# Memory's rows taken into the seven products of the output projection, its token blocks loaded by GpSimd's queue, a new order at its seam, and the rows' squares at other steps

## The reference

```python
h = rms_norm(x, pre_norm)
proj = h @ w_in_a                                  # 1024 -> 3072 + 1536 + 512
p, gate, mq = proj[..., :3072], proj[..., 3072:4608], proj[..., 4608:]
b_gate, c_gate, u = split(p, 3)
mix = b_gate * conv3(c_gate * u)                   # 1024 wide
mem_o = attention(mq, rms_norm(mem, mem_norm) @ w_mem_kv)   # 4 heads, 512 wide
y = (concatenate([mix, mem_o]) * silu(gate)) @ w_out         # 1536 -> 1024
out = x + rms_norm(y, post_norm)
```

## Time and profile before

| what | value |
|---|---|
| three runs, median (lowest to highest) | 2201.29 us (2198.6 to 2203.97) |
| profiled execution, its own time | 2198.74 us |
| its span, first to last instruction | 2197.0 us |
| mean granted TensorE clock | 0.999 |
| instructions | 26714 |
| busy: PE, PEld | 2172.3 us (99%), 1802.3 us (82%) |
| busy: DVE, ACT, POOL | 1174.7 us (53%), 737.3 us (34%), 131.8 us (6%) |
| DMA | 488.47 MB, mean 222 GB/s |
| chain that ended last | PE 91%, DVE 4%, DMA 2%, ACT 2%, issue 1% |

### The profile page before, as it was taken

How to read it: one execution, slowest core, us unless ns; L and a number is a source line. 1 busy time by engine, 2 the same in 40 slices (tenths; PEclk the granted TensorE clock), 3 DMA queues, 4 the chain that set the end, 5 groups by cost and what they waited for, 6 DMA issues and landing times.

```text
span 2197.0 us, 26714 instructions
## 1 busy us (share of the span) xinstructions
PE 2172.3 (99%) x9916; PEld 1802.3 (82%) x9916; DVE 1174.7 (53%) x1847; ACT 737.3 (34%) x1329; POOL 131.8 (6%) x207
## 2 busy tenths in 40 slices
PE   9999999999999999999999999999999999999998
PEld 7888788888888888888888878888887788888887
DVE  7668667643335352254334337585754755555554
ACT  5444333411221341221114334535442533333332
POOL 0000000000000000011000000101010100000000
PEclk9999999999999999999999999999999999999999
DMA  6887777677676777888768666666668633344332
GB/s 240 296 318 274 278 271 271 236 237 282 229 247 211 269 250 261 285 263 300 258 211 274 226 215 202 216 196 216 201 200 303 220 121 109 121 134 134 128 116 73
DMA packets 148336, 488.47 MB, mean 222 GB/s; under 512 B 16688, under 2 KB 16720, under 8 KB 144880
## 3 DMA queue, kind: packets, MB, share of 16 engines
q1 hardware_dynamic: 120672, 387.50, 50.3%
q0 software_dynamic: 27536, 99.27, 14.1%
HBM read 350.38 MB, written 136.33 MB: 222 GB/s over the span
## 4 chain that ended last, share of the span: by engine, by line
PE 91%; DVE 4%; DMA 2%; ACT 2%; issue 1%; SPq 0%; DVEq 0%; ACTq 0%
PE banks L1547 30%; PE banks L1548 30%; PE banks L1549 30%; DVE hop_lo L1171 1%; DMA slots<-w_split 1%; PE banks L1644 1%; ACT hop_hi L891 1%; ACT probs L952 0%; DVE x_in L1157 0%; DMA raws<-in_w_in 0%; DMA raws<-in_w_kv 0%; DVE rmax L1320 0%; DVE pt_lo L1335 0%; DVE slots L1199 0%; ACT slots L846 0%
## 5 line engine op out<-in xcount | busy, mean ns | idle before, releaser
L1547 PE MATMUL banks<-hop_hi,slots 128*128 128x512 f32 x2632 | 1028.4, 391 | 9.6 <-DMA slots<-w_split 4.0
L1548 PE MATMUL banks<-hop_lo,slots 128*128 128x512 f32 x2632 | 1025.2, 390 | 0.0
L1549 PE MATMUL banks<-hop_hi,slots 128*128 128x512 f32 x2632 | 1024.8, 389 | 0.0
L1547 PEld LDWEIGHTS banks<-hop_hi,slots 128*128 128x128 f32 x2632 | 494.6, 188 | 117.5 <-DMA slots<-w_split 7.0
L1549 PEld LDWEIGHTS banks<-hop_hi,slots 128*128 128x128 f32 x2632 | 494.4, 188 | 103.3
L1548 PEld LDWEIGHTS banks<-hop_lo,slots 128*128 128x128 f32 x2632 | 494.7, 188 | 100.3
L1199 DVE TENSOR_TENSOR slots<-raws,slots 128x512 fp32r<-128x512 f32 x156 | 106.8, 690 | 154.9 <-ACT slots L846 154.4
L1251 DVE TENSOR_TENSOR u<-banks,u 128x512 f32<-128x512 f32 x54 | 37.2, 690 | 227.6 <-PE banks L1549 227.6
L902 ACT ACTIVATE s<-banks 128x512 f32<-128x512 f32 x94 | 56.2, 598 | 299.5 <-PE banks L1549 298.7
L846 ACT ACTIVATE slots<-raws 128x512 fp32r<-128x512 f32 x156 | 96.7, 625 | 151.6 <-PE banks L1549 130.9
L846 ACT ACTIVATE slots<-st_w 128x512 fp32r<-128x512 f32 x144 | 90.2, 626 | 149.0 <-PE banks L1549 119.2
(11 more groups left out here) (170 smaller groups left out, 2035.9 us busy)
## 6 DMA issues: line engine op xcount, KB each, us to landing
slots<-w_split SPq DMA_DIRECT2D x406, 512.0 KB, 3.7
w_split<-slots SPq DMA_DIRECT2D x140, 512.0 KB, 3.4
raws<-in_w_in SPq DMA_DIRECT2D x86, 256.0 KB, 4.5
x_in<-in_x_t SPq DMA_DIRECT2D x16, 1024.0 KB, 6.9
g_kept<-mix POOLq DMA_DIRECT2D x32, 512.0 KB, 6.5
raws<-g_kept SPq DMA_DIRECT2D x64, 256.0 KB, 3.9
row<-in_x POOLq DMA_DIRECT2D x24, 512.0 KB, 6.0
x_zb<-in_x POOLq DMA_DIRECT2D x22, 512.0 KB, 4.1
```

Of the source, the lines that this page charges most:

```text
L1547: nc.tensor.matmul(dst, a, c, start=first, stop=False, skip_group_check=True)
L1548: nc.tensor.matmul(dst, a, d, start=False, stop=False, skip_group_check=True)
L1549: return nc.tensor.matmul(dst, b, c, start=False, stop=last, skip_group_check=True)
```

## The change

What it does:

- Memory's four blocks of rows go through the seven products: each has two blocks more (`HB` = 2), 18 matmuls instead of 12. M0, M1, `add_memory` and the adding of its PSUM bank are gone. A token block has 768 columns instead of 512 (`BLOCK`), holds the gated memory output in its last 256, and is kept so in `g_kept`.
- The seven split sums of memory's rows are made in macro 2, one each three steps from step 15 to 57 (`MW_AT`), and kept in `mw_kept`. In the output stage those of R1, R6, R7, R4 stay in SBUF; those of R5, R3, R2 are loaded anew in every pair by SP (`load_stream`), into one buffer of two blocks. R5 takes memory's blocks first, R3 after two others, R2 after three.
- The output stage has three slots for units (`out_slots`) instead of four, and builds them three steps ahead. Token blocks have one buffer each (`out_raws`); sums are made in place.
- Token blocks of all pairs but the first are loaded by POOL (`load_block`), between its stores and residual loads, of which there are two buffers instead of three. ACT evacuates straight into `mix`, when the tile before is finished.
- At the seam all seven operands go through two staging blocks; three of them (R7, R2, R4) are split after the output stage has begun. In its first pair ACT saves R1, R5, R6 in free PSUM banks and copies them later.
- Squares of rows: steps 20, 27, 34, 41 and 54, 60, 66, 72; each row is loaded one step after the square before it. Memory's two squares: steps 108 and 118 of macro 2, its root and inverse there too. The sums of `w_out`'s rows start 14 steps later.

The core of the diff:

```diff
-OUT_ORDER = [R1, R5, R6, R3, M0, R7, R2, M1, R4]
+OUT_STEPS = [(ALL_PAIRS + j, r) for j in range(OUT_PAIRS) for r in range(PRODUCTS)]
+HB = MH // 2
+BLOCK = (HK + HB) * P
+OUT_SLOTS = 3
+STREAMED = {R5: 0, R3: 2, R2: 3}
-SUMS_AFTER = list(range(6, 6 + 2 * HK + 1, 2))
+SUMS_AFTER = list(range(8, 8 + 2 * HK + 1, 2))
+MW_AT = [15 + 3 * n + 3 * (n // PRODUCTS) for n in range(HB * PRODUCTS)]
+MEM_SQUARES = (108, 118)
...
         def prefetch_steps(m):
-            return (41, 52, 63), (69, 80, 91)
+            return ((20, 27, 34, 41), 43, 63), ((54, 60, 66, 72), 74, 91)
...
+            def load_stream(j, r):
+                n = STREAM.index((j, r))
+                for k in range(HB):
+                    if n:
+                        sp.wait_ge(mw_used, HB * (n - 1) + k + 1)
+                    sp.dma_start(mw_stream[:, k, :, :].bitcast(f32), mw_kept[r, k]).then_inc(mw_stream_dma[k], 16)
...
-                    if step == squares - 11:
+                    if step == squares[0] - 6:
                         load_row(tile, 0)
                     for c in range(1, SUB):
-                        if step == squares + 3 * c - 2:
+                        if step == squares[c - 1] + 1:
                             load_row(tile, c)
...
+            for j in range(OUT_PAIRS):
+                if j:
+                    if j + 1 < OUT_PAIRS:
+                        load_block(pool, ALL_PAIRS + j + 1, X21)
+                    store_tile(2 * j - 1)
+                    load_residual(2 * j + 1)
+                if j + 1 < OUT_PAIRS:
+                    for block in (X11, X12, X22) if j else OUT_BLOCKS:
+                        load_block(pool, ALL_PAIRS + j + 1, block)
+                if j == 0:
+                    load_residual(0)
+                    load_residual(1)
+                store_tile(2 * j)
+                if j + 1 < OUT_PAIRS:
+                    load_residual(2 * j + 2)
...
+                if p == ALL_PAIRS and r == R3:
+                    mix_free(act, p, 1)
+                    for first, later, done in ((R6, R3, u2_done), (R5, R7, p5_done), (R1, R2, s1_done)):
+                        act.wait_ge(done, seven_to(p))
+                        nc.scalar.activation(temp(p, later), first_temp[first], ACT.Copy).then_inc(first_mixed, 1)
...
-                    if i == PAIRS - 1 and m + 1 == OUT and r != R4:
-                        operand_hi(OUT, r)
+                    if i == PAIRS - 1 and m + 1 == OUT and r in (R1, R5, R7, R2):
+                        operand_hi(OUT, {R1: R1, R5: R5, R7: R6, R2: R3}[r])
...
+                if n in (0, 2, 3):
+                    operand_hi(OUT, {0: R7, 2: R2, 3: R4}[n])
...
+                if n in (0, 1, 3, 4):
+                    operand_lo(OUT, {0: R3, 1: R7, 3: R2, 4: R4}[n])
...
-                for k in range(HK):
+                tiles = list(range(HK))
+                if m >= OUT:
+                    at = STREAMED.get(r, HK)
+                    tiles[at:at] = range(HK, HK + HB)
+                for k in tiles:
                     w = [a[:, k * P:(k + 1) * P] for a in unit(u)]
-                    op = product(dst, w, [a[:, r, k, :] for a in (hop_hi, hop_lo)], k == 0 and r in starts, k == HK - 1)
+                    y = [a[:, r, k, :] for a in (hop_hi, hop_lo)] if k < HK else memory_rows(p, r, k - HK)
+                    op = product(dst, w, y, k == tiles[0] and r in (R1, R5, R2), k == tiles[-1])
```

476 lines of the change are left out of this document (282 added, 194 removed).

## The result

| kernel | median, us (range) | ratio to before, 95% interval | profiled execution, span |
|---|---|---|---|
| before | 2201.29 (2198.6 to 2203.97) | 1 | 2198.74, 2197.0 |
| changed | 2190.34 (2187.47 to 2196.44) | 0.9948 [0.9932, 0.9963] | 2188.14, 2186.3 |

A forecast was written before the change was run, and what follows sets the result against it. PE, busy in 99% of the span, was taken as the bound, so the number of matmuls sets the time. Terms -21.8 + 5.7 - 6.4 = -22.5 gave 2176.2 (profiled) or 2178.8 (median); forecast 2178, range 2172 to 2184, chance 0.58.

The forecast's parts named there:

- 1. The matmuls: Output stage: 6 fewer matmuls a pair, 96 in all, at 0.2268 us each, -21.8 us.
- 2. Steady state: The 16 pairs of the output stage: added work stays hidden behind PE, pair 28.6 us, cost 0.
- Rival C: Output stage: R5's evacuation late in every pair, each of 15 pairs losing 1 us, 2193; chance 0.06.
- 3. The seam: Entry to the output stage: waits of PE and half clock sum to 7.7 us against 2.0, +5.7 us.
- 4. Squares: Squares spread further apart end PE's waits near 154 and 231 us and before the first keys, -6.4 us.
- 5. Memory's rows in macro tile 3: Making memory's rows there (called macro 2) costs 0; a late load would cost once, up to 3 us.
- 6. Ends: Tail behind the last product and loads at steps 122 to 127: unchanged, 0.
- A: Seam costs no more than now, loads landing in 4 us and DVE catching up: 2173; chance 0.12.
- B: GpSimd's loads come late because DVE works, R4 2 to 4 us later at the seam: 2184 to 2188; chance 0.13.
- D: Output stage: memory's rows late from SP's queue, R2 and R3 waiting in 15 pairs, 28.5 us: 2207; chance 0.05.
- E: The squares don't help, since another load comes late there: 2184; chance 0.06.

The follow-up runs named there:

- e9: Changed kernel with the conv tiles last in SBUF, so mix, R7's memory rows and the first output slot lie on multiples of 1 KB: 2185.59 us, ratio 0.9927.
- e8: Kernel before with only the x rows' squares and their loads at the changed kernel's steps: 2192.93 us, ratio 0.9961.
- e4: Changed kernel with GpSimd loading the raw memory rows in eight spaced pieces of 256 KB instead of two pairs of 512 KB: 2189.25 us.
- e12: Changed kernel loading only 32 of 512 columns of the raw memory rows in macro tile 3, splits and stores kept: 2188.21 us, ratio 0.9939.
- e1: Changed kernel with everything in SBUF behind the conv tiles (mix, R7's rows, first output slot) 32 bytes later: 2190.27 us.
- e2: Changed kernel with SyncE issuing R7's memory rows ahead of R2's operand: 2191.72 us.
- e5: Changed kernel with the tiles behind the conv tiles in another SBUF order, the first output slot 16 KB lower: 2189.33 us.
- e17: Changed kernel with the tiles behind the conv tiles 96 bytes later: 2188.31 us.
- e6: Changed kernel with GpSimd's seam loads (token blocks, post gain) held back and R4's low half ahead of pair 1's first split: 2185.33 us, ratio 0.9922.
- e14: Changed kernel with VectorE's low halves of R6's and R3's operands earlier, plus the edits of e6: 2184.46 us, ratio 0.9927.
- e10: e7 with R4's operand, R2's streamed rows and GpSimd's token blocks also waiting until R2's operand has landed: 2191.22 us.
- e7: Changed kernel with R7's rows ahead of R2's operand, GpSimd's seam loads held back, ScalarE copying R5's result before R7's operand: 2194.22 us.
- e3: Changed kernel with the x rows' squares and their loads back at the steps they had before: 2203.61 us, ratio 1.0011.
- e15: e9 with VectorE's residual sum of the odd token tile ahead of the same step's split: 2194.89 us.

## Why the prediction failed, point by point

**1. The matmuls** (-21.8): 96 fewer at 0.2268. The count held. The price held for two slots of three.

**2. Steady state** (0): wrong by 4.9 us. Waits were looked for and rightly not found: no pair but the first shows a wait of PE. The step that failed is the one before, "a pair becomes 28.6 us": it took the distance of the earlier trace rows for a constant of the matmul, while it depends on where the operands lie. e9 shows 28.56 with the same instructions at other places. Rival C was a true next bound, 2.3 us to spare by the working; in e9 it is used up in a few pairs, and PE waits there.

**3. The seam** (+5.7): the step that failed is the time that loads take to land there, with one load left out altogether. It measured +10.2. R3's wait for ScalarE's copy was 1.1 (1.27 with the restart), forecast 1.4. The half clock cost 2.3, forecast 1.6, at a granted 0.60 and 0.72 in the two stretches behind the stop. The wait of R4, forecast 0.1, was 1.4 (1.6 with the restart). The wait for `hop_lo` of R2, forecast 4.6, did not show, because another stood ahead of it: R7's memory rows, 6.9 us, which the working priced at nothing. It would have shown otherwise, and with some 7 us: R2's operand took 8.7 us to land where the working had 6.2, and its low half was ready 29.2 us into the stage in place of 26.4. The chain of 7.4 us behind that landing was right (7.5 in the working). The working followed three operands, 3 MB, and left out the other 8 MB of the same 31 us (rows of R7 and R4, streams, stores, post gain, blocks), though the sum was to be had from the code: 10.9 MB moved from 1711 to 1742, which at 410 GB/s take 27 of the 31 us. Each load was priced by landings of 5.0 to 6.2 us, measured when the queue was not full. Even the upper bound, 11 us in all, rested on such a landing (6.9), and the seam cost 12.2. The Trainium skill's price ("DMA: Bandwidth & Descriptors", section "Anatomy of one DMA — SWDGE (gpsimd) path") was cited as 4.4 us for 1 MB. It is a fit for one DMA on GpSimd's path, and these are SyncE's loads. R7's operand, issued while the engines stood still, took 5.0 us, near it; with the engines full the next ones took 8.7 to 14.0, so here the price doesn't agree.

**4. Squares** (-6.4): right, and a little small. At the squares themselves it was -5.6 (e8 and the changed kernel) against -5.1. The wait before the first keys, 1.42 in the earlier trace rows, is gone, and the place gives 1.7 against 1.3.

**5. Memory's rows in macro tile 3** (0, up to 3): the bound, not the value. 3.0 us of waits in place of 0.4, and 3.3 us lost with the restarts, for `slots` loads beside 22 GB/s more traffic. That the traffic does it is argued; e4 and e12 only exclude the raw rows' loads as the main cause. The cover that the working checked was ScalarE's and VectorE's; the loads of the units were not on the list.

**6. Ends** (0): held, within 0.2 us behind the last product.

Rivals. A was ruled out: the seam cost 12.2 us. B: GpSimd's blocks of 384 KB took 6.1 us in the median (1760 to 2150), more than the 4.1 of its 512 KB loads before, and no PE wait came of it in the changed kernel's steady state. Whether VectorE's work or the fuller DMA did it was not tried. C didn't occur in the changed kernel. D: memory's streams landed in 4.5 us in the median and didn't hold PE up in the changed kernel; ruled out as a cost of every pair (e1 and e2 have one such wait each, of 0.6 and 0.3 us). E was ruled out by e8.

## What to carry to other kernels

Before pricing a reordered transition load by load, add up its bytes, all queues together, and divide by the rate at which the DMA engines are full: a list of what must land by when shows at once whether the order or the total is the limit, and if it is the total, only fewer bytes or an earlier start help. Then list what the engines still do behind each landing: a second chain may end just behind the one that is seen. A change of buffers is a change of addresses: compare the distance of matmul starts by operand tile before taking it as a constant. And a stage that is faster than its neighbours hides their slack; ask which chain is next before counting a gain in it whole.

## What the hardware showed that was not expected

- **Operands off the raster cost some 16 cycles a matmul.** With all tiles on places equal modulo 1 KB, 128x512 matmuls start 0.2267 us apart (e9). With the first slot 32, 64 or 128 bytes off that raster (changed kernel and e5, e1, e17) those that read it start 0.2330 to 0.2334 us apart, at a granted clock of 1.00; 0.0066 us at 2.4 GHz are 16 cycles. With R7's rows as the operand that is off and the slot even it is 0.2331 (32 bytes), 0.2322 (64) and 0.2319 (128), so it matters little which of the two is off. Where both are, the mean over 10 groups is 0.2290 at 32 bytes each (changed kernel and e5; inside such a stretch the starts are 0.227 apart again), 0.2304 at 64 (e1) and 0.2317 at 128 (e17). So the two operands' relative place alone is not the rule, since it is the same in all of these. What the rule is, the runs don't settle.
- **With the DMA engines full at 410 GB/s, landings take up to nearly three times as long.** 1 MB took 5.0 to 6.2 us in the kernel before, and 8.7, 12.7 and 14.0 here from 1718 on. Loads issued earlier delay one (e6, e14). Loads issued later cost R2's operand 1.4 us (e10 against e7: 10.2 and 11.6 us). But they are not nothing: until R7's rows landed, 7.9 MB had moved since 1711.4, and only 6.2 MB of loads and stores had been issued by 1719.05, these rows included; the other 1.7 MB were issued later, GpSimd's token block of 1720.96 among them, which landed at 1731.48, ahead of the rows of 1719.05. No run held back just these.
- **Waits ride on one queue.** Three times (e3, e15, and e9's last pair) a store or a load that nobody needed yet held up a load that was wanted: GpSimd issued them in the order of the code, and the one ahead waited 14.0, 8.5 and 5.9 us for an engine or a landing.
